# Two attentions worked by pairs of heads, four places for the weights of all: a one-core kernel of two transformer blocks

## The chip, the cores and the metric

One NeuronCore of a Trainium2 chip runs the whole program in one launch. Its engines run side by side and meet at semaphores: TensorE (PE, matmuls into PSUM), VectorE (DVE), ScalarE (ACT), GpSimd (POOL, hardly used here), and SyncE (SP), which issues the DMAs. The metric is the device time of one execution in microseconds, lower is better; the median of three runs stands for the kernel.

## The reference

Two blocks, each of two layers, on 256 tokens of width 1024, all in float32. A mixer is followed by a feed-forward part in each layer. The four mixers are these:

```
stick-breaking (16 heads of 64): z = q k^T / 8;  past = key < query
    log_fail = where(past, log_sigmoid(-z), 0);  later = reversed exclusive cumsum(log_fail)
    a = where(past, exp(log_sigmoid(z) + later), 0);  out = a v
dilated (8 heads of 64, three groups of dilation 1, 4, 16, 256 keys each): banded softmax,
    the groups joined by softmax of their log-sum-exp, which is one softmax over all their keys
latent (8 heads, q and k of width 96, v of 64): 256 context queries over 256 keys,
    and 256 main queries over 512 keys (context and main)
grouped-query (8 heads of 128, 2 key-value heads): 256 queries over 512 keys
```

## The kernel before

Activations are kept with the feature on the 128 partitions and the token along the free axis. Most of the time goes to projections ("linear" phases): a weight chunk comes by DMA into one of three places of `raw`, ScalarE copies it into `whi` (a rounded high part), VectorE subtracts it into `wlo` (the rest), and TensorE multiplies high and low parts. Phases follow one another in a list; every engine walks the same list in its own block of code (`@block.tensor`, `@block.scalar`, `@block.vector`), in an order written out by hand. `at(family, key)` names the semaphore and the value that tells of an event, `own()` the engine's own last event. A linear behind an attention waits until all three engines have ended that attention. During an attention no weight chunk is split, and hardly any DMA runs.

The attention phases are the kinds "stick" and "softmax". In both, PSUM's eight banks (`ps[:, b, :]`, 512 floats a partition) hold scores in the low banks and finished products in the high ones.

*stick* goes through 16 heads. TensorE: `z(hd)` computes the scores, keys on the partitions and queries along the free axis (256 + 128 columns, as later queries only see the second half of the keys), into bank hd % 4. ScalarE: `ex(hd)` takes Abs, Exp and Ln (L1369, L1371, L1375). VectorE: `fail(hd)` makes the fail terms in `sbf` (L1851, L1855). TensorE then adds the sums over later keys into the same bank, by three matmuls with constant triangles (tiles `sbf,squares` in the trace). ScalarE: Exp into `sba` (L1393). VectorE: `mask(hd)` (L1863). TensorE: `attend(hd)` multiplies with v into bank 4 or 5, the even head on partitions 0 to 63 and the odd head on 64 to 127. When a pair of heads is done, ScalarE's `high(pair)` (L1381) copies it into `uh` and VectorE's `low(pair)` (L1868) subtracts the rest into `ul`. `sbt`, `sbe`, `sbl`, `sbf` and `sba` have two places each. The scores and v matmuls read 64 rows or write 64 columns of the array.

*softmax* goes through units, each 128 queries of one head: 16 units in the dilated attention ("dil", 384 or 768 keys, masked), 32 in the latent one ("mla", 16 of 256 keys and then 16 of 512), 16 in the grouped-query one ("gqa", 512 keys). Queries stand on the partitions. For unit n: TensorE `scores` (two heads at a time but for gqa), VectorE `max_` (L1902 and L1904, or L1896 with mask), ScalarE `exp_` (L1413, with the row sum) into `pr`, VectorE `norm_` (L1911, L1913), TensorE `turn` (L984, transposes of 128 x 128), ScalarE `copy_` (L1425) into `pt`, TensorE `attend`, two heads at a time. After four units of mla, two heads are complete ("ends"): ScalarE `high_` (L1433), VectorE `low_` (L1920). `pr` has three places, `pt` four, `small` holds the maxima and sums in two sets. All fp32 matmuls go through `mm` (L686), which is why one line stands for them. ScalarE and VectorE work in this order:

```
ScalarE: exp_(0); for n: exp_(n+1), copy_(n), high_(n-3) where that unit ends a pair
VectorE: max_(0); for n: max_(n+1), norm_(n), low_(n-4) where that unit ends a pair
TensorE, mla: scores(0), scores(1); for pair m: turn x2, scores(m+2), attend(m-1)
```

## Time and profile before

| | us |
|---|---|
| median of 3 runs | 1884.77 (1883.54 to 1887.55) |
| the profiled execution | 1886.12 |
| its span, first to last instruction | 1884.3 |
| TensorE busy | 1747.8 (93%) |
| VectorE busy | 1245.6 (66%) |
| ScalarE busy | 878.5 (47%) |
| mean granted TensorE clock | 0.972 of full |

The profile is of one execution. Busy times count instructions that compute; a wait, or the issue of a DMA, is idle. PE's times are modelled from starts, so a busy PE isn't PE at its peak. In a window's row, the stretch and its length are followed by the busy us of PE, PEld (weight loads), DVE, ACT and POOL, each with its number of instructions, then PEclk, the DMA share and GB/s; PEclk is the share of the full TensorE clock of 2.4 GHz that was granted (0.50 is 1.2 GHz). In a timeline's row stand the start, the duration of the group that was merged into it, the engine, the line, and `out<-in` by tile name; the brackets give the idle time before it and who ended it. An fp32 matmul shows as two records.

### The profile page before, as it was taken

What the parts mean: (1) busy time and instruction counts of PE and PEld (TensorE: products, weight loads), DVE (VectorE), ACT (ScalarE), POOL (GpSimd) and SP (SyncE); (2) the same over time, 40 slices, a digit from 0 to 9 for tenths busy, and PEclk for the clock granted to TensorE, in tenths of its full rate; (3) what the DMA queues carried; (4) which work ended last, traced back from release to release, by engine and by line L of the source; (5) the groups of instructions that cost most, each with busy time, mean ns of one, the idle gap of its engine ahead of it and who ended that gap; (6) DMA issues with size and microseconds to landing.
All of it is one profiled execution on the core that took longest, in us unless ns stands there. A gap on an engine that the chain in (4) does not pass through costs nothing.

```text
span 1884.3 us, 25106 instructions
## 1 busy us (share of the span) xinstructions
PE 1747.8 (93%) x9870; PEld 1458.6 (77%) x9870; DVE 1245.6 (66%) x1539; ACT 878.5 (47%) x1113; POOL 0.2 (0%) x4
## 2 busy tenths in 40 slices
PE   6998999989997899988988799999999988999998
PEld 4876788978885688887656477887888876789997
DVE  4855778757885677855356646878566665577764
ACT  5464554454335455335535635333233354565552
POOL 0000000000000000000000000000000000000000
PEclk9999999989999899998998999999999989999999
DMA  5922367734650356743104022555644513035551
GB/s 178 309 80 90 121 193 240 245 111 160 220 183 1 117 181 203 230 135 104 36 17 129 1 95 85 170 164 175 229 157 145 190 60 125 1 117 194 183 184 63
DMA packets 240471, 264.75 MB, mean 141 GB/s; under 512 B 7007, under 2 KB 218978, under 8 KB 240354
## 3 DMA queue, kind: packets, MB, share of 16 engines
q1 hardware_dynamic: 238658, 258.90, 42.1%
q10 hardware_dynamic: 1696, 4.26, 0.7%
q8 instruction: 78, 1.28, 0.3%
q14 instruction: 39, 0.32, 0.1%
HBM read 262.08 MB, written 1.05 MB: 140 GB/s over the span
## 4 chain that ended last, share of the span: by engine, by line
PE 79%; DVE 10%; ACT 8%; issue 2%; DMA 1%; DVEq 0%; ACTq 0%
PE ps L686 77%; ACT y L1315 2%; DVE wlo L1492 1%; ACT u L1318 1%; PE ps L984 1%; ACT whi L1057 1%; DVE y L1779 1%; DVE u L1772 1%; DVE small L1902 1%; DMA xin<-in_ctx 1%; DVE y L1711 1%; DVE rstd L1675 1%; DVE rstd L1677 1%; DVE y L1796 1%; ACT pt L1425 1%
## 5 line engine op out<-in xcount | busy, mean ns | idle before, releaser
L686 PE MATMUL ps<-u,whi 128*128 128x512 f32 (+2 forms) x3408 | 899.3, 347 | 33.3 <-DVE u L1772 15.6
L686 PEld LDWEIGHTS ps<-u,whi 128*128 128x128 f32 (+1 forms) x3408 | 593.0, 192 | 135.6 <-issue 25.7
L686 PE MATMUL ps<-u,wlo 128*128 128x256 f32 (+1 forms) x2084 | 646.9, 310 | 0.0
L1492 DVE TENSOR_TENSOR wlo<-raw,whi 128x2048 fp32r<-128x2048 f32 (+6 forms) x212 | 454.1, 2142 | 227.4 <-ACT whi L1057 220.3
L1057 ACT ACTIVATE whi<-raw 128x2048 fp32r<-128x2048 f32 (+6 forms) x212 | 381.1, 1798 | 233.8 <-PE ps L686 214.9
L686 PEld LDWEIGHTS ps<-u,wlo 128*128 128x128 f32 x2084 | 399.2, 192 | 20.8
L686 PE MATMUL ps<-hid,whi 128*128 128x512 f32 (+1 forms) x1212 | 353.7, 364 | 0.0
L686 PE MATMUL ps<-hid,wlo 128*128 128x256 f32 (+1 forms) x864 | 261.9, 303 | 0.0
L686 PEld LDWEIGHTS ps<-hid,whi 128*128 128x128 f32 x1212 | 216.3, 189 | 40.6 <-issue 3.4
L686 PEld LDWEIGHTS ps<-hid,wlo 128*128 128x128 f32 x864 | 163.5, 189 | 7.0
L1711 DVE SCALAR_TENSOR_TENSOR y<-idle_half,cc,y 128x1024 f32<-128x1024 f32 x70 | 89.9, 1285 | 5.3 <-DVE wlo L1492 0.5
L1239 ACT ACTIVATE cacc<-ps,convv 128x512 f32<-128x512 f32 (+1 forms) x44 | 29.6, 674 | 107.2 <-PE ps L686 106.3
L686 PE MATMUL ps<-squares 128*128 128x256 f32 (+1 forms) x308 | 72.1, 388 | 0.0
L686 PE MATMUL ps<-sq,squares 128*128 128x256 f32 (+1 forms) x108 | 45.7, 577 | 26.5 <-ACT sq L1119 17.1
L686 PEld LDWEIGHTS ps<-squares 128*128 128x128 f32 x308 | 59.0, 194 | 9.8 <-issue 1.9
L686 PE MATMUL ps<-whi,u 128*128 128x512 f32 (+1 forms) x224 | 65.6, 374 | 0.0
L1156 ACT ACTIVATE work<-ps 128x512 f32<-128x512 f32 x38 | 22.7, 599 | 91.5 <-PE ps L686 91.4
L1249 ACT ACTIVATE csil<-cacc 128x512 f32<-128x512 f32 (+1 forms) x44 | 23.2, 528 | 87.6 <-PE ps L686 85.1
L984 PE MATMUL ps<-squares,pr 128*128 128x128 f32 x232 | 39.8, 296 | 23.5 <-DVE pr L1913 18.5
L1772 DVE TENSOR_TENSOR u<-y,u 128x256 fp32r<-128x256 f32 (+1 forms) x80 | 40.4, 505 | 26.7 <-ACT u L1318 21.7
L686 PEld LDWEIGHTS ps<-sq,squares 128*128 128x128 f32 x108 | 24.7, 251 | 42.8 <-issue 29.6
L1425 ACT ACTIVATE pt<-ps 128x512 f32<-128x512 f32 (+2 forms) x72 | 37.1, 515 | 42.9 <-PE ps L984 41.3
(228 smaller groups left out, 1617.0 us busy)
## 6 DMA issues: line engine op xcount, KB each, us to landing
raw<-in_ffn_w_up SPq DMA_DIRECT2D x44, 1024.0 KB, 5.1
raw<-in_w_ff_in SPq DMA_DIRECT2D x32, 1024.0 KB, 5.3
raw<-in_w_ff_out SPq DMA_DIRECT2D x32, 1024.0 KB, 5.2
modw<-in_w_mod SPq DMA_DIRECT2D x112, 256.0 KB, 3.8
idle_half<-in_w_mod SPq DMA_DIRECT2D x80, 256.0 KB, 3.4
raw<-in_w_in_dil SPq DMA_DIRECT2D x18, 1024.0 KB, 5.1
raw<-in_w_in_sb SPq DMA_DIRECT2D x12, 1024.0 KB, 7.4
raw<-in_w_ple_gate SPq DMA_DIRECT2D x8, 1024.0 KB, 5.2
```

The source lines that it names most:

```text
L686: return pe.matmul(out_, lhsT, rhs, start=start, stop=stop, skip_group_check=True)
L984: last = pe.transpose(ps[:, (4 + k // 4) if wide else 4 + n % 2, (k % 4) * P:(k % 4 + 1) * P], pr[:, n % 3, k * P:(k + 1) * P], ident)
L1057: nc.scalar.activation(whi[:, s % SPLIT, 0:n], raw[:, c["r"] % RAW, 0:n], ACT.Copy).then_inc(*up("weights_high", s))
L1156: nc.scalar.activation(half_sum(p, c), halves_of(c)[1], ACT.Copy, scale=HD ** -0.5 if kind == "qk1" and g < 4 else 1.0).then_inc(*up("half ...
L1239: nc.scalar.activation(cacc[:, j, 0:T], A_[:, j, :], ACT.Identity, bias=convv[:, l, 66 + f:67 + f], scale=convv[:, l, 22 + f:23 + f]).then ...
L1249: nc.scalar.activation(csil[:, j, 0:T], cacc[:, j, 0:T], ACT.Silu).then_inc(*up("gated_silu", (i, g - 1, j)))
L1315: nc.scalar.activation(y[:, k, sl], y[:, k, sl], ACT.Identity, bias=mod_at(l, which, k, s_), scale=mod_at(l, which + 1, k, s_)).then_inc(* ...
L1318: nc.scalar.activation(dst[:, k_, 0:p["T"]], y[:, p.get("s0", 0) + k, 0:p["T"]], ACT.Copy).then_inc(*up("operand_high", (i, k)))
L1425: nc.scalar.activation(pt[:, n % 4, c0:c0 + w], ps[:, (4 + c0 // 512) if u["mask"] is not None else 4 + n % 2, 0:w], ACT.Copy).then_inc(*u ...
L1492: nc.vector.tensor_tensor(wlo[:, s % SPLIT, 0:n], raw[:, c["r"] % RAW, 0:n], whi[:, s % SPLIT, 0:n].bitcast(F32), ALU.subtract).then_inc(* ...
L1711: nc.vector.scalar_tensor_tensor(total, mod_weights(m), cc[:, k, v:v + 1], total, ALU.mult, ALU.add).then_inc(*up("mod_taken", m["n"]))
L1772: nc.vector.tensor_tensor((cl if c else ul)[:, k_, 0:T], y[:, s0 + k, 0:T], (ch if c else uh)[:, k_, 0:T].bitcast(F32), ALU.subtract).then ...
```

## The change

In the stick-breaking attention TensorE's `z` and `attend` take a pair of heads j, the matmuls of the two heads alternating. Scores go through six banks and products into banks 6 and 7. `sbl` and `sbf` get three places, `sba` four. ScalarE runs `ex` two heads ahead of the weights' Exp where it ran one ahead, VectorE `fail` two ahead of `mask`. `high` and `low` of a pair come later: `high` after an even head, `low` after an odd one.

In the latent attention (`step = 2`) ScalarE does two `exp_`, then two `copy_`, then `high_` of the pair before; VectorE two `max_`, then `low_`, then two `norm_`; TensorE issues the scores of pair m + 2 ahead of the turns of pair m. The dilated and grouped-query attentions keep their order (`step = 1`). For all three `pr` gets a fourth place and `small` four sets, so `exp_` and `max_` wait for what lies four units back, not two or three. `pt` keeps four places, of which the fourth is now the tile `work`. No instruction is added or taken away.

```diff
-        sbl = arena("sbl", [P, 2, 384], 30 * K)
-        sbf = arena("sbf", [P, 2, 384], 33 * K)
-        sba = arena("sba", [P, 2, 384], 36 * K)
+        sbl = arena("sbl", [P, 3, 384], 30 * K)
+        sbf = arena("sbf", [P, 3, 384], 35 * K)
+        sba = arena("sba", [P, 4, 384], 40 * K)
...
-        pr = arena("pr", [P, 3, 768], 41 * K)
-        pt = arena("pt", [P, 4, 768], 50 * K)
+        pr = arena("pr", [P, 4, 768], 41 * K)
+        pt3 = arena("pt", [P, 3, 768], 53 * K)
...
+        pt = [pt3[:, n, :] for n in range(3)] + [work[:, :, :, :].rearrange("p a b c -> p (a b c)")]
+    def z(j):
+
+        for hd in (2 * j, 2 * j + 1):
+            if hd >= 6:
+                pe.wait_ge(*at("stick_weights", (i, hd - 6)))
+        for keys in range(2):
+            for hd in (2 * j, 2 * j + 1):
+                o, b = (hd % 2) * 64, hd % 6
+                qh = q1[o:o + 64, j, :]
+                if keys == 0:
+                    mm(ps[:, b, 0:256], k1[o:o + 64, j, 0:P], qh, True, False)
+                else:
+                    mm(ps[:, b, 256:384], k1[o:o + 64, j, P:S], qh[:, P:S], False, True).then_inc(*up("scores", (i, hd)))
+
+    def attend(j):
+
+        for hd in (2 * j, 2 * j + 1):
+            pe.wait_ge(*at("masked", (i, hd)))
+        if j >= 2:
+            pe.wait_ge(*at("operand_low", (i, j - 2)))
+        for keys in range(2):
+            for hd in (2 * j, 2 * j + 1):
+                o = (hd % 2) * 64
+                vv = v1[:, keys, hd * 64:(hd + 1) * 64]
+                if keys == 0:
+                    mm(ps[o:o + 64, 6 + j % 2, 0:256], vv, sba[:, hd % 4, 0:256], True, False)
+                else:
+                    mm(ps[o:o + 64, 6 + j % 2, 128:256], vv, sba[:, hd % 4, 256:384], False, True).then_inc(
+                        *up("attended", (i, hd)))
...
-    for hd in range(HEADS):
-        if hd + 2 < HEADS:
-            z(hd + 2)
...
-        if hd >= 1:
-            attend(hd - 1)
-    attend(HEADS - 1)
+    for j in range(HEADS // 2):
+        for hd in (2 * j, 2 * j + 1):
+            b, zb = hd % 3, hd % 6
+            pe.wait_ge(*at("fail_ready", (i, hd)))
+            mm(ps[:, zb, 0:256], negtri, sbf[:, b, 0:256], False, False)
+            mm(ps[:, zb, 128:256], negones, sbf[:, b, 256:384], False, False)
+            mm(ps[:, zb, 256:384], negtri, sbf[:, b, 256:384], False, True).then_inc(
+                *up("fail_summed", (i, hd)))
+        if j + 2 < HEADS // 2:
+            z(j + 2)
+        if j >= 1:
+            attend(j - 1)
+    attend(HEADS // 2 - 1)
...
-    ahead = 1 if wide else 4 // heads_of
+    ahead = dict(mla=2, dil=1, gqa=4)[p["what"]]
...
-        if wide and m + 1 < M:
-            scores(m + 1)
+        if p["what"] != "gqa" and m + ahead < M:
+            scores(m + ahead)
         for u in units[m * heads_of:(m + 1) * heads_of]:
             turn(u)
-        if not wide and m + ahead < M:
+        if p["what"] == "gqa" and m + ahead < M:
             scores(m + ahead)
...
-        if hd >= 2:
-            act.wait_ge(*at("fail_ready", (i, hd - 2)))
-        act.wait_ge(*own())
-        nc.scalar.activation(sbl[:, b, :], sbe[:, b, :], ACT.Ln, bias=1.0).then_inc(
+        if hd >= 3:
+            act.wait_ge(*at("fail_ready", (i, hd - 3)))
+        act.wait_ge(*own())
+        nc.scalar.activation(sbl[:, hd % 3, :], sbe[:, b, :], ACT.Ln, bias=1.0).then_inc(
             *up("weights_exp", (i, hd)))
...
     ex(0)
+    ex(1)
     for hd in range(HEADS):
-        if hd + 1 < HEADS:
-            ex(hd + 1)
-        b = hd % 2
+        if hd + 2 < HEADS:
+            ex(hd + 2)
         act.wait_ge(*at("fail_summed", (i, hd)))
-        if hd >= 2:
-            act.wait_ge(*at("attended", (i, hd - 2)))
-        act.wait_ge(*own())
-        nc.scalar.activation(sba[:, b, :], ps[:, hd % 4, 0:384], ACT.Exp).then_inc(*up("stick_weights", (i, hd)))
-        if hd % 2 == 1 and hd >= 3:
-            high(hd // 2 - 1)
+        if hd >= 4:
+            act.wait_ge(*at("attended", (i, hd - 4)))
+        act.wait_ge(*own())
+        nc.scalar.activation(sba[:, hd % 4, :], ps[:, hd % 6, 0:384], ACT.Exp).then_inc(*up("stick_weights", (i, hd)))
+        if hd % 2 == 0 and hd >= 4:
+            high(hd // 2 - 2)
+    high(HEADS // 2 - 2)
     high(HEADS // 2 - 1)
...
-        if n >= 3:
-            act.wait_ge(*at("turned", (i, n - 3)))
...
+        if n >= 4:
+            act.wait_ge(*at("turned", (i, n - 4)))
...
-    exp_(units[0])
-    for n in range(N):
-        if n + 1 < N:
-            exp_(units[n + 1])
-        copy_(units[n])
-        if n >= 3 and units[n - 3]["ends"]:
-            high_(units[n - 3])
-    for n in (N - 3, N - 2, N - 1):
-        if units[n]["ends"]:
-            high_(units[n])
+    step, lag = (2, 1) if p["what"] == "mla" else (1, 3)
+    for u in units[0:step]:
+        exp_(u)
+    for n in range(0, N, step):
+        for u in units[n + step:n + 2 * step]:
+            exp_(u)
+        for u in units[n:n + step]:
+            copy_(u)
+        if n >= lag and units[n - lag]["ends"]:
+            high_(units[n - lag])
+    for u in units[N - lag:]:
+        if u["ends"]:
+            high_(u)
...
-        if hd >= 2:
-            dve.wait_ge(*at("fail_summed", (i, hd - 2)))
...
+        if hd >= 3:
+            dve.wait_ge(*at("fail_summed", (i, hd - 3)))
...
     past2 = squares[:, 7:8, :].to_broadcast([P, 2, P])
     fail(0)
+    fail(1)
     for hd in range(HEADS):
-        if hd + 1 < HEADS:
-            fail(hd + 1)
+        if hd + 2 < HEADS:
+            fail(hd + 2)
         mask(hd)
-        if hd % 2 == 0 and hd >= 4:
+        if hd % 2 == 1 and hd >= 5:
             low(hd // 2 - 2)
     low(HEADS // 2 - 2)
     low(HEADS // 2 - 1)
...
-        if n >= 2:
-            dve.wait_ge(*at("weights_exp", (i, n - 2)))
+        if n >= 4:
+            dve.wait_ge(*at("weights_exp", (i, n - 4)))
         if u["mask"] is not None:
-            if n >= 3:
-                dve.wait_ge(*at("turned", (i, n - 3)))
+            if n >= 4:
+                dve.wait_ge(*at("turned", (i, n - 4)))
...
-    max_(units[0])
-    for n in range(N):
-        if n + 1 < N:
-            max_(units[n + 1])
-        norm_(units[n])
-        if n >= 4 and units[n - 4]["ends"]:
-            low_(units[n - 4])
-    for n in (N - 4, N - 3, N - 2, N - 1):
-        if units[n]["ends"]:
-            low_(units[n])
+    step, lag = (2, 3) if p["what"] == "mla" else (1, 4)
+    for u in units[0:step]:
+        max_(u)
+    for n in range(0, N, step):
+        for u in units[n + step:n + 2 * step]:
+            max_(u)
+        if step == 2 and n >= lag and units[n - lag]["ends"]:
+            low_(units[n - lag])
+        for u in units[n:n + step]:
+            norm_(u)
+        if step == 1 and n >= lag and units[n - lag]["ends"]:
+            low_(units[n - lag])
+    for u in units[N - lag:]:
+        if u["ends"]:
+            low_(u)
```

Old `z` and `attend` stand above. The rest renames places in the same way (`n % 3` to `n % 4`, `hd % 4` to `hd % 6`, `pt[:, n % 4, ...]` to `pt[n % 4][...]`, the columns of `small`, banks 4 and 5 to 6 and 7).

## Rows read from the trace of the kernel before

**Rows 1.** The page's chain that ended last: share of the span by engine.

```profile
PE 79%; DVE 10%; ACT 8%; issue 2%; DMA 1%; DVEq 0%; ACTq 0%
```

**Rows 2.** Busy us per engine in three attention stages: stick-breaking, latent, grouped-query.

```profile
105.20:155.70 50.50, 45.91 (x224) 33.97 (x225) 25.93 (x56) 36.16 (x73) 0.00 (x0) 0.93 0.05 18
...
1019.70:1089.40 69.70, 56.78 (x352) 34.69 (x352) 46.35 (x138) 40.88 (x105) 0.00 (x0) 0.88 0.04 15
1608.30:1648.00 39.70, 36.92 (x226) 27.65 (x227) 27.34 (x72) 26.03 (x57) 0.00 (x0) 1.00 0.00 1
```

**Rows 3.** Timeline, stick-breaking: ScalarE's first instruction, then one head (start, us, what).

```profile
106.19 0.49 ACT L1369 ACTIVATE sbt<-ps 128x384 f32<-128x384 f32 x1 [1.07 <-PE ps L686]
...
126.59 0.38 ACT L1381 ACTIVATE u<-ps 128x256 fp32r<-128x256 f32 x1
126.69 0.92 PE L686 MATMUL ps<-q,k 64*128 64x256 f32 x4
127.07 0.49 ACT L1369 ACTIVATE sbt<-ps 128x384 f32<-128x384 f32 x1
127.54 1.14 PE L686 MATMUL ps<-sbf,squares 128*128 128x256 f32 x6
...
128.61 0.86 PE L686 MATMUL ps<-sba,v 128*64 128x256 f32 x4
...
128.84 0.49 ACT L1393 ACTIVATE sba<-ps 128x384 f32<-128x384 f32 x1
...
129.41 0.92 PE L686 MATMUL ps<-q,k 64*128 64x256 f32 x4
129.43 0.49 ACT L1369 ACTIVATE sbt<-ps 128x384 f32<-128x384 f32 x1
```

**Rows 4.** Windows with the granted clock (PEclk): stick-breaking, dilated, latent.

```profile
109.50:116.00 6.50, 6.50 (x20) 4.74 (x19) 2.81 (x6) 3.67 (x8) 0.00 (x0) 0.50 0.00 0
...
575.00:600.00 25.00, 18.02 (x188) 13.79 (x186) 15.34 (x50) 16.81 (x38) 0.00 (x0) 1.00 0.00 1
1022.00:1033.80 11.80, 11.01 (x36) 7.03 (x34) 7.86 (x30) 6.55 (x21) 0.00 (x0) 0.50 0.03 9
```

**Rows 5.** Timeline of VectorE, latent stage, one 512-wide unit.

```profile
1064.43 0.69 DVE L1902 TENSOR_REDUCE small<-ps 128x1 f32<-128x512 f32 x1
...
1065.41 0.16 DVE L1911 RECIPROCAL small<-small 128x1 f32<-128x1 f32 x1
...
1066.23 0.69 DVE L1902 TENSOR_REDUCE small<-ps 128x1 f32<-128x512 f32 x1
```

**Rows 6.** The maxima's line between 1047 and 1084: duration ns min/median/max, first and last start.

```profile
L1902 DVE TENSOR_REDUCE small<-ps x16: 691/692/693, 1047.3 to 1082.9; 128x1 f32<-128x512 f32 x16
```

**Rows 7.** Who waited for whom between 1047 and 1084: us, times, longest.

```profile
DVE u L1920 <- ACT u L1433: 6.9, 4, 2.7
```

**Rows 8.** Timeline of TensorE, latent stage, one pair of 512-wide units.

```profile
1064.84 1.88 PE L686 MATMUL ps<-km,qm 96*128 96x512 f32 x4
1066.65 1.09 PE L686 MATMUL ps<-pt,vm 128*64 128x128 f32 x16
1067.68 1.09 PE L984 MATMUL ps<-squares,pr 128*128 128x128 f32 x8
1068.61 1.88 PE L686 MATMUL ps<-km,qm 96*128 96x512 f32 x4
```

**Rows 9.** Timeline of TensorE, stick-breaking: first scores, then the slow start.

```profile
105.26 1.54 PE L686 MATMUL ps<-q,k 64*128 64x256 f32 x12 [1.21 <-ACT v L1182]
108.90 1.64 PE L686 MATMUL ps<-sbf,squares 128*128 128x256 f32 x6 [2.09 <-DVE sbf L1855]
...
112.04 2.07 PE L686 MATMUL ps<-sbf,squares 128*128 128x256 f32 x6
114.04 1.54 PE L686 MATMUL ps<-sba,v 128*64 128x256 f32 x4
```

**Rows 10.** The chain in order of time: the last Ln of stick-breaking.

```profile
149.92 0.53 ACT sbl L1375
```

More of the change, by code:

```diff
@@ L918, in attend @@
-                    def attend(hd):
-                        b = hd % 2
-                        pe.wait_ge(*at("masked", (i, hd)))
-                        pair, o = hd // 2, (hd % 2) * 64
-                        if pair >= 2 and hd % 2 == 0:
-                            pe.wait_ge(*at("operand_low", (i, pair - 2)))
-                        dst = ps[o:o + 64, 4 + pair % 2, 0:S]
-                        vv = [v1[:, t, hd * 64:(hd + 1) * 64] for t in range(2)]
-                        mm(dst[:, 0:256], vv[0], sba[:, b, 0:256], True, False)
-                        mm(dst[:, 128:256], vv[1], sba[:, b, 256:384], False, True).then_inc(
-                            *up("attended", (i, hd)))
@@ L983, in turn @@
                         for k in range(kt):
-                            last = pe.transpose(ps[:, (4 + k // 4) if wide else 4 + n % 2, (k % 4) * P:(k % 4 + 1) * P], pr[:, n % 3, k * P:(k + 1) * P], ident)
+                            last = pe.transpose(ps[:, (4 + k // 4) if wide else 4 + n % 2, (k % 4) * P:(k % 4 + 1) * P], pr[:, n % 4, k * P:(k + 1) * P], ident)
                         last.then_inc(*up("turned", (i, n)))
@@ L1424, in copy_ @@
                             act.wait_ge(*own())
-                            nc.scalar.activation(pt[:, n % 4, c0:c0 + w], ps[:, (4 + c0 // 512) if u["mask"] is not None else 4 + n % 2, 0:w], ACT.Copy).then_inc(
+                            nc.scalar.activation(pt[n % 4][:, c0:c0 + w], ps[:, (4 + c0 // 512) if u["mask"] is not None else 4 + n % 2, 0:w], ACT.Copy).then_inc(
                                 *up("turned_copied", (i, n)))
@@ L1900, in max_ @@
+                                    -u["scale"], small[:, 8 + b:9 + b] if c0 else -NEG, ALU.add, ALU.min,
+                                    accum_out=small[:, b:b + 1] if c0 + w == W else small[:, 8 + b:9 + b]).then_inc(*up("max_ready", (i, n)))
                         else:
                             dve.wait_ge(*own())
-                            nc.vector.tensor_reduce(small[:, 4 + b:5 + b], ps[:, n % 4, 0:W], AX.X, ALU.max).then_inc(*up("vector_step"))
+                            nc.vector.tensor_reduce(small[:, 8 + b:9 + b], ps[:, n % 4, 0:W], AX.X, ALU.max).then_inc(*up("vector_step"))
```

51 lines of the change are left out of this document (16 added, 35 removed).

## The prediction

> **What bounds the kernel now.** I read the page's chain first: TensorE holds 79% of it [rows 1], so time is won only where TensorE waits, or where it is shortened itself. Then the busy time of the attention stages [rows 2], which are all that the change touches. Outside them nothing is edited; inside them the DMA share is 0 to 5%, so no transfer can be late. The grouped-query stage has TensorE busy 36.9 of 39.7 us: it is bound there. The others have it idle or at the lower clock for part of the time: stick-breaking 45.9 of 50.5 at a mean clock of 0.93, latent 56.8 of 69.7 at 0.88, and the dilated one 18.0 of the 25 in its middle [rows 4].
>
> In the stick-breaking stage the timelines [rows 3] give the steady state. TensorE runs scores (126.69), tail sums (127.54), products with v (128.61) and the next scores (129.41) without a break: 2.72 us a head, 5.43 a pair. ScalarE's own work is a little less: Abs, Exp and Ln take 1.77 (127.07 to 128.84), the weights' Exp 0.59 (to 129.43), and the copy of a finished pair 0.48 (126.59 to 127.07). That is 2 x 2.36 + 0.48 = 5.20 a pair. So TensorE bounds, with ScalarE 4% behind. At the start it is slower: the clock stands at 1.2 GHz from 109.5 to 116 [rows 4], after TensorE had stood from the end of the first scores (106.8) to 108.9 for head 0's Ln and fail terms [rows 9].
>
> In the latent stage VectorE sets the pace of the 512-wide units: max and its scaling 0.98 (1064.43 to 1065.41), reciprocal and scaling 0.82 (to 1066.23), so 1.80 a unit [rows 5]. But the sixteen maxima from 1047.3 to 1082.9 [rows 6] lie 2.37 apart. The waits say where the rest is: 6.9 us in four waits for ScalarE's copy of a finished pair [rows 7]. That copy waits for the products with v, and these stand on TensorE behind the scores: scores 1.81, products 1.03, two turns 0.93 [rows 8], 3.77 a pair.
>
> **The change part by part.** *Stick-breaking, TensorE.* The matmuls of two heads now alternate and use different halves of the array (64 rows for the scores, 64 columns for v). The trace shows the effect already: the scores of heads 0, 1 and 2, issued one after the other, took 1.54 us for three [rows 9], not 3 x 0.85. Two overlapped and one alone give about 0.7 + 0.85. I take 0.85 for a pair of scores (a wait included) and 0.85 for a pair's products, and 1.07 for each tail sum: 3.84 a pair. Bounds: no overlap at all, 2 x (0.85 + 1.07 + 0.80) = 5.43 less two waits saved; full overlap, 3.8. Below 5.20 ScalarE is the bound, so even poor overlap leaves most of the gain.
>
> *Stick-breaking, ScalarE.* Six score banks, three places for Ln and for the fail terms and four for the weights let ScalarE run two heads ahead. Between the end of a head's Ln and its weights' Exp now lie about 4.7 us of other ScalarE work; the path through VectorE (1.0) and TensorE (1.1, or 2.0 at the lower clock) is shorter, so ScalarE should not wait. It starts at 106.19 [rows 3]. Up to the end of the last Ln it has 16 x 1.77 + 13 x 0.59 + 5 x 0.48 = 38.4 us, so 144.6. Walking the first heads with the matmuls at 1.2 GHz (tail sums 2.0, 112.04 to 114.04; scores about as the products of one head, 1.5; [rows 9]) adds 0.3: 144.9. Now it is 149.92 + 0.53 = 150.45 [rows 10]: 5.5 us gained. From there to the next linear at 155.7 the chain is the same (fail terms, sums, Exp, mask, products, copy, subtraction), plus one thing: the subtraction of pair 5 now stands behind the mask of head 15 on VectorE, and the last products wait for it, +0.5. **Stick-breaking: -5.0.** Of it 1.3 to 1.9 is the steady state (0.12 a head), the rest the idle of ScalarE at the start. Bounds: -1 (waits eat the lead) and -6.
>
> *Stick-breaking, the clock.* TensorE will be busy 3.84 of 5.20 us, 74%, in pieces with waits of up to about a microsecond. The nearest rows are the dilated stage: busy 18.0 of 25 us (72%) from 575 to 600, with the granted clock at 1.00 [rows 4], that is 2.4 GHz. I take it to hold. The Trainium skill, "TensorE: Matmul & The Clock Gate", section "A second HAM failure mode: psum-queue depth-cycling", speaks against this: small idles between groups that cycle through PSUM banks can make the clock swing between its levels. The dilated row does not show it there, but such a drop comes in the rows of other stages; what it would cost is the last rival.
>
> *Latent.* Two maxima, then the subtraction, then two norms; two exponentials, then two copies; scores ahead of the turns. The work is the same, instruction for instruction. The copy of a finished pair now comes while VectorE does the next two maxima (2 x 0.98), which covers turn, copy and products after the norms (0.5 + 0.6 + 1.0). So four 512-wide units cost 4 x 1.80 + 0.56 (subtraction with its gaps) + 0.1 left of the wait = 7.9, or 1.97 a unit; TensorE's 3.77 a pair stays just under 3.94. From unit 16's maximum to unit 30's: 14 x 1.97 = 27.6, and to unit 31's 28.6, where now it is 35.6. The end gets longer: after the last maxima come two norms of the pair before (1.6), then the subtraction waits for turn, copy, products and copy (2.5) with no maxima to cover it, then the last two norms (1.6), turn, copy, products, copy, subtraction (3.5). From unit 31's maximum to the next linear that is 10.3; now 1089.4 - 1082.8 = 6.6. So -7.0 + 3.7 = -3.3. In the 256-wide half TensorE runs at 1.2 GHz until 1033.8, busy 11.0 of 11.8 us [rows 4]: the order can change nothing much. After it about two waits for the pair's copy go, at half of the 1.7 us (6.9 / 4) that they cost above: -1.7 at most, 0 at least; I take -1.2 for both and the order at the start. **Latent: -4.5**, between 0 (the lengthened end and new waits eat it) and -7.
>
> *Dilated and grouped-query.* Order and work stay. Four places for the weights let a maximum start before the turn of three units back. By VectorE's order that turn has nearly always ended by then, so I allow **-0.2**, between 0 and -1: the maxima of the stage are few (16), and each could come earlier only until it waits for its scores. Grouped-query is bound by TensorE, whose work is untouched: 0. What hides the moved fourth place of the turned weights is nothing: it is an address. If a linear's use of that tile met the attention, it would wait; the stages are apart.
>
> Sum: 5.0 + 3.3 + 1.2 + 0.2 = 9.7. The profiled execution took 1886.12 (span 1884.3, 1.8 around it), so 1876.4; it lies 1.35 above the median 1884.77, so **1875** for the median. Behind each stage comes a linear that waits for it, with TensorE as its bound, so the gain should pass through whole.
>
> **Rivals.** *The latent stage gives nothing.* The subtraction stands before the norms and waits for a copy that waits for products; if that wait (2.5 us without cover, at the end) shows between the pairs too, 0.6 us a pair over the eight wide pairs eats the 4.5. For: TensorE and VectorE are within 4% of each other, so there is no slack to catch up. Against: the maxima cover 2.0 of it. Time: 1884.8 - 5.2 = 1879.6.
> *The stick-breaking stage gives little.* VectorE takes fail (hd+2) before mask (hd), so a late Ln holds the mask, the products and the bank. Against: VectorE has 25.9 of 50.5 us to do. With -1 there: 1879.1; with the latent stage at nothing as well, 1883.6, which is no change.
> *Slower: the clock.* If with more idle TensorE stays at 1.2 GHz in the stick-breaking stage, a pair costs 2 x 2.0 for the tail sums and 2 x 1.5 for scores and products (a head's took 1.54 at that clock, and an overlapped pair takes about as long as one head) [rows 9]: 7.0 instead of 5.20. Eight pairs from 108.9, where the first tail sums start, end at 164.9, and the next linear comes at 166.1 instead of 155.7, +10.4; with -4.7 elsewhere 1890.5. For: it fell there before. Against: it came back at 116 with the same instructions running back to back, as they will again. Each pair at the lower clock costs 1.8; with six the whole gain is gone, with eight the kernel is slower by over 0.2%.
>
> **How the numbers follow.** Both stages gain as above: 0.64, times 1871 to 1879. Latent at nothing 0.16 (1879.6), stick-breaking at little 0.08 (1879 to 1881), both at nothing 0.06 (about 1884), the clock 0.06 (1890.5). Beyond the likeliest the range takes the two one-sided cases, up to 1881; its lower end is both stages at their better bounds, -6 and -7 with some gain in the clock, near 1870. 0.2% (3.8 us) is about what a measurement of this kernel can tell from no change; 1881.0 is that border. Faster: 0.64 + 0.16 + about half of the third case = 0.84; same 0.10; slower 0.06.
>
> **What would show it.** Stick-breaking: next linear near 150.6, ScalarE without idle before its Exp (L1393's line) from 107 on, TensorE with 0.5 to 1 us of idle a pair; two score matmuls starting within 0.05 us. Latent: wide maxima in twos, 3.9 us from pair to pair, VectorE's waits for the pair's copy under 2 us in all but for one at the end; stage 65 instead of 69.7 long. Grouped-query unchanged to 0.2. Wrong if: pairs over 5.3 us in the first, a granted clock of 0.5 there after 117, or a wait of over 0.6 us for the copy at each second pair.

## The result, and the profile after

The changed kernel takes 1873.68 us, the median of six runs (1872.44 to 1875.26); the kernel before took 1884.15 beside it (1882.09 to 1887.55). The ratio is 0.9943, with a 95% interval from 0.993 to 0.9956: faster by 10.5 us. The prediction was 1875, in a range from 1870 to 1881.

The profiled execution took 1872.93 us, with a span of 1871.1: 13.2 less than the profiled span before. That pair overstates the gain, as the profiled execution of before lay 2.0 above its median and that of after 0.75 below its own: 13.2 - 2.75 = 10.5. Since durations come from the profiles, the terms below are compared there.

Windows of the stick-breaking and the latent stage, to be read beside [rows 2]:

```profile
105.00:149.70 44.70, 32.51 (x224) 25.15 (x225) 25.91 (x56) 36.02 (x73) 0.00 (x0) 0.96 0.06 20
...
1010.30:1073.50 63.20, 54.91 (x352) 33.24 (x352) 46.33 (x138) 40.74 (x105) 0.00 (x0) 0.95 0.05 16
```

In the stick-breaking stage TensorE's busy time fell from 45.9 to 32.5 us with the same instructions, VectorE's and ScalarE's did not move, and the stage is 5.8 shorter. In the latent stage all busy times stay about as they were (56.8 to 54.9 for TensorE, at a higher clock): what went is idle time.

A stage is measured in the traces from TensorE's first instruction in it to the first one of the next linear:

| us | before | after | difference | predicted |
|---|---|---|---|---|
| stick-breaking | 50.46 | 44.69 | -5.77 | -5.0 |
| latent: first maximum to the 17th | 25.90 | 22.42 | -3.48 | -1.2 |
| latent: 17th maximum to the 32nd | 35.56 | 28.73 | -6.83 | -7.0 |
| latent: 32nd maximum to the next linear | 6.60 | 10.41 | +3.81 | +3.7 |
| latent, whole | 69.72 | 63.23 | -6.49 | -4.5 |
| dilated | 49.21 | 49.03 | -0.18 | -0.2 |
| grouped-query | 39.27 | 39.23 | -0.04 | 0 |

That is 12.5 of the 13.2. The other 0.7 is what is left of larger differences in stretches that were not edited: the linears between the dilated and the latent stage took 405.4 us where they had taken 409.1, those between the latent and the grouped-query one 521.4 against 518.9. The same 409.1 came down to 405.5 in a kernel below with the old latent attention (`stick_only`), so this is scatter. The dilated stage scatters too: with the new places and one and the same list it took from 46.0 to 51.3 us in the kernels below, its mean granted clock being 0.96 and 0.80 there. Its -0.18 says nothing.

**Stick-breaking.** Timeline after, one pair of heads and ScalarE's first instruction, to be read beside [rows 3]:

```profile
105.96 0.49 ACT L1378 ACTIVATE sbt<-ps 128x384 f32<-128x384 f32 x1 [1.07 <-PE ps L687]
...
123.23 0.49 ACT L1402 ACTIVATE sba<-ps 128x384 f32<-128x384 f32 x1
...
124.22 1.14 PE L687 MATMUL ps<-sbf,squares 128*128 128x256 f32 x6 [1.29 <-DVE sbf L1868]
...
125.29 0.92 PE L687 MATMUL ps<-q,k 64*128 64x256 f32 x8
...
126.15 0.87 PE L687 MATMUL ps<-sba,v 128*64 128x256 f32 x8
...
128.41 0.49 ACT L1402 ACTIVATE sba<-ps 128x384 f32<-128x384 f32 x1
```

The scores of two heads now take 0.92 us, as those of one did before (x8 against x4 records for the same duration); their products take 0.87. From 123.23 to 128.41 is the period of a pair: 5.18, where TensorE's loop gave 5.43. TensorE now waits (1.29 before the sums at 124.22), and ScalarE does not. The bound has passed from TensorE to ScalarE.

The chain at the end of the same stage (start, us, engine, tile and line):

```profile
143.33 0.53 ACT sbl L1384
...
146.66 0.43 DVE sba L1876
...
147.19 0.44 DVE u L1881
...
147.76 0.89 PE ps L687 x8
...
149.73 0.47 PE ps L687
```

The last Ln ends at 143.86, against 150.45 before [rows 10]. Behind it the mask (146.66) is followed by the subtraction of an earlier pair (147.19), and only then come the last products.

**Latent.** Timeline of VectorE, one pair of 512-wide units: two maxima, the first of two norms, and the next pair's maximum:

```profile
1046.01 0.69 DVE L1916 TENSOR_REDUCE small<-ps 128x1 f32<-128x512 f32 x1
...
1047.02 0.69 DVE L1916 TENSOR_REDUCE small<-ps 128x1 f32<-128x512 f32 x1
...
1048.00 0.16 DVE L1925 RECIPROCAL small<-small 128x1 f32<-128x1 f32 x1
...
1049.60 0.69 DVE L1916 TENSOR_REDUCE small<-ps 128x1 f32<-128x512 f32 x1
```

In such a step nothing but the instructions' own gaps is left: 3.59 a pair. Every other step has the subtraction too, and takes 4.13 to 4.48 from 1041.9 on: 0.56 for the subtraction, up to 0.46 for a wait for ScalarE's copy. The maxima's line in two stretches (number, ns min/median/max, first and last start), and the wait for the pair's copy from 1034 to 1072, which answers to [rows 7]:

```profile
L1916 DVE TENSOR_REDUCE small<-ps x17: 423/425/692, 1012.0 to 1034.4; 128x1 f32<-128x256 f32 x16, 128x1 f32<-128x512 f32 x1
...
L1916 DVE TENSOR_REDUCE small<-ps x15: 691/692/692, 1035.4 to 1063.1; 128x1 f32<-128x512 f32 x15
...
DVE u L1934 <- ACT u L1443: 3.1, 3, 2.2
```

The 512-wide maxima lie (1063.1 - 1034.4) / 15 = 1.91 apart, 2.37 before [rows 6]. Of the waits for the copy one long one is left, 2.2 us. It stands in the lengthened end, which the chain shows in order of time:

```profile
1063.13 0.70 DVE small L1916
...
1065.10 0.50 DVE pr L1927
...
1067.40 0.39 ACT u L1443
...
1067.82 0.43 DVE u L1934
...
1069.33 0.50 DVE pr L1927
...
1073.55 0.47 PE ps L687
```

From the norm's end at 1065.60 the chain leaves VectorE for turns, products and copy and comes back at 1067.82 for the subtraction. The last two norms start only behind it. That they could have started earlier is shown below, by the kernel that does them first.

**The clock.** Windows of after (the slow stretch of stick-breaking, its middle, the slow stretch of the latent stage), then the slow stretch of the latent stage before, beside [rows 4]:

```profile
110.50:113.90 3.40, 3.40 (x15) 2.60 (x15) 1.96 (x4) 2.96 (x6) 0.00 (x0) 0.50 0.00 0
...
116.00:142.00 26.00, 20.11 (x148) 15.26 (x147) 16.33 (x36) 22.27 (x46) 0.00 (x0) 1.00 0.01 1
...
1011.70:1018.40 6.70, 6.37 (x16) 4.45 (x16) 5.05 (x19) 3.77 (x13) 0.00 (x0) 0.50 0.19 64
```

```profile
1020.80:1034.40 13.60, 12.20 (x43) 8.06 (x44) 9.38 (x34) 6.83 (x22) 0.00 (x0) 0.50 0.12 42
```

From 116 to 142 the stick-breaking stage keeps 2.4 GHz with TensorE busy 20.1 of 26 us. In the latent stage the clock is back after 6.8 us (at 1018.4), where it took 13.7 before.

### The profile page after: what moved, and what is told of

It is laid out like the page before. It is cut to its first block, busy times and chain, and to the rows that moved or that the text cites. A ratio compares the mean times of both kernels' runs of the same rounds, so it can differ in the third digit from the quotient of the medians.

```text
span 1871.1 us, 25111 instructions
## 1 busy us (share of the span) xinstructions
PE 1732.7 (93%) x9870; PEld 1449.5 (77%) x9870; DVE 1245.3 (67%) x1539; ACT 876.8 (47%) x1113; POOL 0.2 (0%) x4
## 4 chain that ended last, share of the span: by engine, by line
PE 77%; DVE 10%; ACT 9%; issue 2%; DMA 1%; DVEq 0%; ACTq 0%
PE ps L687 75%; ACT y L1324 2%; DVE wlo L1505 1%; ACT u L1327 1%; PE ps L993 1%; ACT whi L1066 1%; DVE y L1792 1%; DVE u L1785 1%; DVE pr L1927 1%; DVE small L1916 1%; DVE y L1724 1%; DMA xin<-in_ctx 1%; DVE rstd L1688 1%; DVE rstd L1690 1%; DVE y L1809 1%
## 5 line engine op out<-in xcount | busy, mean ns | idle before, releaser
L993 PE MATMUL ps<-squares,pr 128*128 128x128 f32 x232 | 39.7, 295 | 18.3 <-DVE pr L1927 12.5
L1595 DVE SCALAR_TENSOR_TENSOR cacc<-ps,convv,cacc 128x510 f32<-128x510 f32 (+1 forms) x44 | 27.1, 615 | 43.8 <-ACT cacc L1248 40.8
```

The source lines that it names most:

```text
L993: last = pe.transpose(ps[:, (4 + k // 4) if wide else 4 + n % 2, (k % 4) * P:(k % 4 + 1) * P], pr[:, n % 4, k * P:(k + 1) * P], ident)
L1595: nc.vector.scalar_tensor_tensor(a[:, :, 1:S], x[:, :, 0:S - 1], convv[:, l, f:f + 1], a[:, :, 1:S], ALU.mult, ALU.add).then_inc(*up("vect ...
```

## The experiments

Twelve kernels were run, each timed against the kernel before on the same chip. "Stage" is the length as in the table above.

**Each half alone.** The first kernel has the new stick-breaking attention and the old softmax attentions, the second the reverse.

> The change in the stick-breaking attention alone; the softmax attentions as before. If the stages gain apart from each other, the stick-breaking stage is 44.7 us long as after (50.5 before), the latent stage stays at 69 to 70, and the time is 5.8 us under before. If the earlier return of the clock or the earlier end in one stage helps the other, the latent stage shortens here too, by 1 us or more.

> The change in the softmax attentions alone; stick-breaking as before. If the stages gain apart, stick-breaking stays at 50.5 us, the latent stage is 63.2 as after (69.7 before), and the time is 6.5 us under before. The rival, that half of the latent gain is the clock's phase and not the order, gives 65 to 68 for the latent stage here, since the stage starts 5.8 us later.

```diff
# stick_only: the softmax attentions' lists as before
+                    max_(units[0])
+                    for n in range(N):
...
# latent_only: stick's lists, places and banks as before
-                        if hd + 2 < HEADS:
-                            ex(hd + 2)
+                        if hd + 1 < HEADS:
+                            ex(hd + 1)
```

Stick-breaking alone: 1878.89, ratio 0.9968 (0.9952 to 0.9984), its stage 45.50, the latent one 69.67. Latent alone: 1881.79, 0.9982 (0.9967 to 0.9996), its stage 63.23 to the hundredth as in the full change, stick-breaking 50.48. In the profiles the halves don't touch each other, and the ratios multiply to 0.995, within the interval of the full change. The times are less clear than the stages: the first half gives 6.2 us against the 1885.04 beside it, as expected (5.8), the second 3.3 where its stage gives 6.5 and 6.5 was expected; even the end of its interval, 0.9967, is only 6.2. Single times of that kernel run from 1871.3 to 1884.6, and no run tells where the rest went.

The first kernel's stick-breaking stage is 0.8 longer than the full change's (45.50 against 44.69), though the same lists run there. The last Ln ends as long after ScalarE's first instruction in both (37.9); the difference lies behind it, where in this run the clock fell, and not at the start:

```profile
109.90:145.40 35.50, 25.91 (x182) 20.02 (x182) 21.72 (x48) 30.48 (x63) 0.00 (x0) 1.00 0.01 1
145.40:148.80 3.40, 3.22 (x16) 2.11 (x17) 1.90 (x5) 1.09 (x3) 0.00 (x0) 0.50 0.00 0
```

There everything waits for TensorE's last sums and products, which no other work covers.

**A lead of one head, not two.** Banks, places and pairs stay; only ScalarE and VectorE run one head ahead as before.

```diff
-                    ex(1)
...
-                        if hd + 2 < HEADS:
-                            ex(hd + 2)
+                        if hd + 1 < HEADS:
+                            ex(hd + 1)
...
-                    fail(1)
...
-                        if hd + 2 < HEADS:
-                            fail(hd + 2)
+                        if hd + 1 < HEADS:
+                            fail(hd + 1)
```

> After, with ScalarE and VectorE one head ahead in stick-breaking as they were before; TensorE's pairs, banks and places stay. If the gain is ScalarE's lead of two heads, ScalarE waits again for the tail sums (VectorE 1.0 and TensorE 1.1 to 2.8 against 2.4 to 2.8 of its own work): a pair costs 5.4 to 6.2 us instead of 5.2 and the stage 47 to 53. If the gain is TensorE's shorter work by pairs, the lead doesn't matter and the stage stays under 46.

1875.9, ratio 0.9955 (0.9936 to 0.9975), stage 48.34. Timeline of ScalarE's weights' Exp in the slow start, in the middle and for the last head, and windows of the two stretches at the lower clock:

```profile
115.34 0.49 ACT L1401 ACTIVATE sba<-ps 128x384 f32<-128x384 f32 x1 [1.34 <-PE ps L687]
...
122.86 0.49 ACT L1401 ACTIVATE sba<-ps 128x384 f32<-128x384 f32 x1
...
128.05 0.49 ACT L1401 ACTIVATE sba<-ps 128x384 f32<-128x384 f32 x1
...
149.07 0.49 ACT L1401 ACTIVATE sba<-ps 128x384 f32<-128x384 f32 x1 [2.13 <-PE ps L687]
```

```profile
109.20:116.00 6.80, 6.36 (x22) 5.20 (x23) 3.34 (x8) 4.55 (x10) 0.00 (x0) 0.50 0.00 0
...
146.70:150.10 3.40, 3.14 (x14) 2.35 (x14) 1.06 (x3) 0.73 (x2) 0.00 (x0) 0.50 0.00 0
```

The stage came out as expected, the pair did not: the steady pair takes 5.19 with either lead, so one head is enough at 2.4 GHz. Of the 3.65 us by which the stage is longer than after's, part is the clock of this run. It was down for 6.8 us at the start, where after had 3.4; the kernel `low_after`, further down, has the lead of two and the same 6.8, and takes 45.03. And it fell again from 146.7 on, which by the end of the stage (6.80 from the last Ln to the next linear, 5.88 in after) costs some 0.9. That leaves about 2.4 for the second head of lead, an estimate. ScalarE's waits tell where: with one head of lead it waits 2.4 us before the first three weights' Exp (0.59, 0.44 and 1.34), with two heads and the same 6.8 us at the lower clock 0.5 (`low_after`); the other 0.6 lies at the end, where the last head's work starts later.

**Pairs without alternation.** The new loops, but each head's two matmuls issued together.

```diff
-                        for keys in range(2):
-                            for hd in (2 * j, 2 * j + 1):
+                        for hd in (2 * j, 2 * j + 1):
+                            for keys in range(2):
```

> After, with the scores and the products with v of a pair issued head by head, not alternating. If the two halves of the array overlap without alternation, as the first three scores of before seem to show (1.54 us for three), nothing changes: stage 44.7. If overlap needs the alternation, a pair of scores takes 1.3 to 1.6 us instead of 0.85; ScalarE then still bounds (TensorE about 5.0 of 5.2 us a pair), and the stage grows by under 2 us.

1873.48, ratio 0.994 (0.9924 to 0.9956), stage 44.73. Timeline, one pair:

```profile
125.31 0.93 PE L687 MATMUL ps<-q,k 64*128 64x256 f32 x8
...
126.17 0.88 PE L687 MATMUL ps<-sba,v 128*64 128x256 f32 x8
```

0.93 and 0.88 where alternation gives 0.92 and 0.87. The two halves of the array overlap in either order; what counts is that nothing stands between the two heads.

**Is it order or clock?** Matmuls with unused results were put ahead of the first tail sums and of the latent scores, in the kernels after and before.

```diff
+            def idle(n):
+                for _ in range(n):
+                    mm(ps[:, 5, 0:S], ones, squares[:, 0:2, :].rearrange("p j c -> p (j c)"), True, True)
...
                     z(1)
+                    idle(4)
...
+                    if p["what"] == "mla":
+                        idle(6)
```

> After, with idle matmuls (results unused) in the two places where TensorE stands ahead of the stages: 4 after the first scores of stick-breaking, 6 ahead of the first scores of the latent stage; they are there to keep the clock at 2.4 GHz. If stick-breaking is bound by ScalarE even while the clock is down, its stage stays at 44.7 (within 0.4) although the clock stays up. In the latent stage TensorE bounds while the clock is down (1012 to 1018), so it is 1 to 3 us shorter. If the matmuls don't hold the clock, nothing changes.

> The same idle matmuls in the kernel before. There TensorE bounds stick-breaking, so a clock that stays up gives 3 to 4 us in that stage (50.5 to about 47) and 2 to 5 in the latent one (69.7). If stick-breaking before was held by something else at its start, it gains under 1 us. It also tells how much of the change's gain was the time at the lower clock: the change should be worth only about 2 us in stick-breaking against this kernel.

Windows of the stick-breaking stage, after with idle matmuls, then before with them:

```profile
104.90:149.60 44.70, 33.12 (x232) 25.56 (x233) 25.93 (x56) 36.04 (x73) 0.00 (x0) 1.00 0.06 21
```

```profile
104.30:151.60 47.30, 44.68 (x233) 33.34 (x233) 25.93 (x56) 36.11 (x73) 0.00 (x0) 1.00 0.05 19
```

Both hold the full clock throughout. After stays at 44.69: the 3.4 us at the lower clock in its own run had cost nothing, as ScalarE bounds there too. Before falls from 50.46 to 47.29. So 2.6 of the gain of 5.8 is order at the full clock, and 3.2 is what the lower clock at the start had cost the old order. The new order is nearly, but not wholly, proof against it: in `low_after` and `turns_first`, below, the same stick-breaking lists ran with 6.8 us at the lower clock, as in before, and took 45.03 and 45.04. The window of the former:

```profile
110.10:116.90 6.80, 6.38 (x25) 5.02 (x24) 4.12 (x10) 5.68 (x12) 0.00 (x0) 0.50 0.01 2
```

In the latent stage the idle matmuls did harm, against both expectations: 65.06 and 71.09. The clock fell later instead of earlier, and in after with idle matmuls for longer:

```profile
1016.90:1027.10 10.20, 9.94 (x39) 6.12 (x38) 6.54 (x24) 5.12 (x17) 0.00 (x0) 0.50 0.01 2
```

Whole kernels: 1875.85, ratio 0.9935 (0.9919 to 0.9952), and 1880.38, 0.996 (0.9944 to 0.9976).

A second try spread idle matmuls over the first pairs of the latent stage, so as to keep its clock up in both kernels.

```diff
                     for m in range(ahead):
+                        if p["what"] == "mla":
+                            idle((6, 1)[m])
                         scores(m)
+                    if p["what"] == "mla":
+                        idle(3)
...
                             attend(m - 1)
+                        if p["what"] == "mla" and m < 3:
+                            mm(ps[:, 7, 0:S], ones, squares[:, 0:2, :].rearrange("p j c -> p (j c)"), True, True)
```

> After, with idle matmuls in TensorE's gaps of the first narrow units of the latent stage (6 ahead of the first scores, 1 between, 3 behind, 1 in each of the first three steps), to keep the clock at 2.4 GHz there. If the clock stays up, the narrow part (first to seventeenth maximum) is 21.5 to 22.4 us (22.4 after): VectorE bounds it. The idle matmuls themselves may cost up to 1 us.

> The same idle matmuls in the kernel before. If half of what the change gained in the narrow part (25.9 to 22.4) is the clock, which came back after 6 instead of 13 us, the narrow part is 23.5 to 24.5 here. If all of it is the order, it stays near 25.9 with the clock up; if all is the clock, it is 22.4.

After: 1875.91, 0.9948 (0.993 to 0.9967), stage 64.64; its first half is 22.43, at the full clock, where after has 22.42 with the low one for 6.8 us near its start. So that half is bound by VectorE, and that fall costs it nothing. (The later and longer fall of the first try did cost: 24.22.) The stage is still 1.4 longer than after's, all of it in the end (11.80 against 10.41), where the clock now fell for 3.4 us from 1068.7. Before: 1886.72, 1.0012 (0.9997 to 1.0028), stage 67.52, first half 25.37. Windows of the latter:

```profile
1019.70:1035.00 15.30, 13.10 (x76) 9.45 (x78) 11.59 (x38) 8.34 (x27) 0.00 (x0) 1.00 0.18 62
1035.00:1040.00 5.00, 3.46 (x24) 2.18 (x20) 3.91 (x16) 2.68 (x9) 0.00 (x0) 0.78 0.00 0
```

The attempt was only partly clean: the clock fell at 1037.8 for 3.4 us, and the pair behind it took 5.10 us, where the same pair of the kernel before takes 3.67 at full clock. Without the 1.4, the old order at full clock takes 23.9, an estimate. Of the 3.5 that the first half gained, then, 25.9 - 23.9 = 2.0 had been the clock's and 23.9 - 22.4 = 1.5 the order's.

**One engine's order alone.** In the latent stage first TensorE's old order (turns ahead of scores) under the new lists of the others, then the reverse.

```diff
# turns_first
-                        if p["what"] != "gqa" and m + ahead < M:
+                        if wide and m + ahead < M:
                             scores(m + ahead)
...
-                        if p["what"] == "gqa" and m + ahead < M:
+                        if not wide and m + ahead < M:
                             scores(m + ahead)
# scores_first
-                    step, lag = (2, 1) if p["what"] == "mla" else (1, 3)
+                    step, lag = 1, 3
...
-                    step, lag = (2, 3) if p["what"] == "mla" else (1, 4)
+                    step, lag = 1, 4
```

> After, with TensorE's order in the latent stage as before: turns, scores two pairs ahead, products; ScalarE and VectorE stay at pairs. If TensorE's order is a needed part of the gain, the scores now come behind the turns of norms that VectorE does after two maxima, VectorE waits about 1.4 us a pair for scores, and the stage is 66 to 72 us long. If only the order on ScalarE and VectorE matters, it stays at 63 to 64.

> After, with ScalarE's and VectorE's order in the latent stage as before (one unit at a time) and TensorE's scores ahead of the turns: the other half of the latent edit alone. If the two orders only work together, each copy waits behind scores and holds the next exponential, the scores wait for that one, and a wide pair takes about 5.1 us instead of 4.6 before and 3.9 after: stage 72 to 76. If TensorE's order alone brings the products forward and with them the pair's copy, a pair takes 3.9 and the stage 60 to 63.

Turns first: 1899.37, ratio 1.0063 (1.0047 to 1.0079), slower than before, stage 91.61. Scores first: 1906.75, 1.0117 (1.0099 to 1.0136), stage 95.17. The latent window of the first, and its timeline of both engines around one pair:

```profile
1008.70:1100.30 91.60, 69.18 (x353) 39.98 (x353) 46.32 (x138) 40.80 (x105) 0.00 (x0) 0.74 0.03 11
```

```profile
1064.08 0.69 DVE L1916 TENSOR_REDUCE small<-ps 128x1 f32<-128x512 f32 x1 [1.61 <-PE ps L687]
...
1066.82 1.45 PE L993 MATMUL ps<-squares,pr 128*128 128x128 f32 x8 [0.89 <-DVE pr L1927]
1068.10 1.88 PE L687 MATMUL ps<-km,qm 96*128 96x512 f32 x4
...
1069.16 0.69 DVE L1916 TENSOR_REDUCE small<-ps 128x1 f32<-128x512 f32 x1 [1.61 <-PE ps L687]
```

A closed ring: the turns wait for the norms (0.89), the scores stand behind the turns, and the next two maxima wait for these scores (1.61). This pair takes 5.08. Every second pair has the subtraction too; two of these that ran at full clock take 5.61 and 5.95. The other kernel has a ring of its own, in which the scores wait for an exponential that ScalarE runs too late; its latent window and a start of scores:

```profile
1014.40:1109.60 95.20, 68.73 (x352) 43.58 (x353) 46.34 (x138) 40.78 (x105) 0.00 (x0) 0.73 0.03 11
```

```profile
1074.51 1.95 PE L687 MATMUL ps<-km,qm 96*128 96x512 f32 x4 [2.29 <-ACT pr L1423]
```

There a pair takes 5.02 at full clock, and one in which a copy and a subtraction fall due 6.79 (from the maximum at 1067.48 to the one at 1074.27). So in the mean a pair takes longer than the 5.0 and 5.1 on which the expectations went, and the stages are longer than their upper ends, 72 and 76. Two things had been left out: these pairs, and the clock, at 0.74 and 0.73 in the mean. The clock's part can't be told apart exactly. TensorE is busy 14.3 and 13.8 us longer than in after for the same instructions (54.91 there); if that is what the lower clock adds, an estimate, then no more than half of the 28.4 and 31.9 us by which the stages are longer than after's is the clock, and the rest is waits. VectorE's and ScalarE's orders and TensorE's gain only together.

**The subtraction and its wait.** First the subtraction is put behind the norms throughout, then only in the last step of the latent stage, with stick-breaking's last-but-two subtraction ahead of the last mask.

```diff
# low_after
-                        if step == 2 and n >= lag and units[n - lag]["ends"]:
-                            low_(units[n - lag])
                         for u in units[n:n + step]:
                             norm_(u)
-                        if step == 1 and n >= lag and units[n - lag]["ends"]:
+                        if n >= lag and units[n - lag]["ends"]:
                             low_(units[n - lag])
# tails
+                        if hd == HEADS - 1:
+                            low(hd // 2 - 2)
                         mask(hd)
-                        if hd % 2 == 1 and hd >= 5:
+                        if hd % 2 == 1 and 5 <= hd < HEADS - 1:
                             low(hd // 2 - 2)
...
-                        if step == 2 and n >= lag and units[n - lag]["ends"]:
+                        ahead_of_norm = step == 2 and n + step < N
+                        if ahead_of_norm and n >= lag and units[n - lag]["ends"]:
                             low_(units[n - lag])
...
-                        if step == 1 and n >= lag and units[n - lag]["ends"]:
+                        if not ahead_of_norm and n >= lag and units[n - lag]["ends"]:
                             low_(units[n - lag])
```

> After, with VectorE's subtraction of a finished pair behind the two norms in every step of the latent stage, not ahead of them. The steps with a subtraction take 4.46 us after (3.6 without); 0.56 of it is the subtraction, 0.3 the rest of the wait for ScalarE's copy. If the wait is real, it goes: 4.16, the wide part 1 us shorter (28.7 to 27.7) and the end 8.4 instead of 10.4, stage about 60.2. If TensorE is by then the bound of these steps, they stay at 4.4 and only the end gains (61.2).

> After, with the last pair's subtraction moved in both stages: in the latent one behind the last two norms, in stick-breaking the subtraction of pair 5 ahead of the mask of head 15. By the prediction's steps this takes the uncovered wait (about 2.2 us) out of the latent end and 0.5 us out of the stick-breaking end: stages 61.0 and 44.2 instead of 63.2 and 44.7. If the ends are bound elsewhere (ScalarE's copies, TensorE), neither moves by over 0.3.

Behind throughout: 1870.99, ratio 0.9927 (0.9912 to 0.9943), latent stage 62.31, of which 28.41 in the 512-wide part (28.73 after) and 9.81 at the end (10.41). Of the 1.0 expected in the wide part only 0.3 came, in one step. There had been waits to remove, 0.46 and 0.41 us for the copy in two steps of after. The second is gone; in place of the first a wait of 0.46 stands ahead of a norm (1054.89), and the profile names no other engine that ended it. The end got 0.6 shorter and not the 2.0 of the kernel below. The clock fell in it (a fall there cost 1.4 in two other kernels, 11.8 against 10.41); a window of this kernel's last units:

```profile
1070.00:1075.60 5.60, 4.47 (x47) 3.60 (x43) 0.85 (x2) 2.53 (x5) 0.00 (x0) 0.76 0.00 0
```

Only in the last step: **1870.65, ratio 0.9899 (0.9882 to 0.9917)**, latent stage 61.23, its end 8.40, stick-breaking 44.57. The chain at the end of both stages:

```profile
145.95 0.43 DVE sba L1876
...
146.48 0.43 DVE u L1881
...
147.01 0.44 DVE sba L1876
...
1069.34 0.16 DVE small L1920
...
1070.59 0.50 DVE pr L1929
```

In the latent stage the last norms now follow the last maxima at once (1069.34, then 1070.59), and 2.0 us are gone. In stick-breaking the move gave 0.12: mask, subtraction and mask stand back to back from 145.95 on, so the subtraction has only changed its place in a full queue. This version is faster than the kernel before, and its ratio's interval lies below that of the change, though the two were not run side by side. The medians differ by 3.0 us (1873.68 and 1870.65), of which the stages explain 2.1; the kernel before stood at 1886.72 beside it, 2.6 higher than beside the change, so the ratio flatters it a little.

## Why the prediction was right, point by point

**What bounds.** Right for both stages, in their steady state. Stick-breaking passed from TensorE at 5.43 a pair to ScalarE at 5.18 (predicted 5.20); the latent wide part to VectorE, whose maxima take 27.7 us from the 17th to the 31st (predicted 27.6).

**Stick-breaking, -5.0: measured -5.77.** From ScalarE's first instruction to the end of the last Ln were predicted 144.9 - 106.19 = 38.7 and came 143.86 - 105.96 = 37.9. The instructions add up to 0.5 less. The 0.3 of waits from the walk did not come either, but only because the clock of this run was down for 3.4 us. The walk had the first heads' matmuls at the lower clock as in before, where it was down for 6.8, and the two kernels with 6.8 have these waits: 0.35 longer to the last Ln, stage 45.03 and 45.04. The end was put at +0.5: it is (149.73 - 143.86) - (155.7 - 150.45) = +0.6. That two heads overlap without alternation was the reading of [rows 9], and the run without it bears that out. The prediction gave 1.3 to 1.9 of the gain to the steady state and the rest to the start; with the full clock throughout, the kernels differ by 2.6, so the rest, 3.2, was the price of the lower clock at the start.

**The clock there.** Held where the prediction looked, as taken from the dilated row: 20.1 busy of 26 at 1.00. The Trainium skill ("TensorE: Matmul & The Clock Gate", section "A second HAM failure mode: psum-queue depth-cycling"), which was weighed against it, tells of a bf16 kernel whose clock swings between its levels as TensorE idles shortly between groups that cycle through PSUM banks. No swing shows from 116 to 142 here. But the forecast held with some luck: in two kernels with the same stick-breaking lists, `stick_only` and `scores_first`, the clock fell for 3.4 us from 145.4 and 145.2, which the prediction had named as a sign of being wrong (0.5 after 117). It cost 0.8 and 0.9 us of stage, not the 1.8 a pair of the rival. In the two kernels with one engine's order alone the clock did swing: TensorE busy 69.2 of 91.6 and 68.7 of 95.2, and a mean of 0.74 and 0.73.

**Latent, wide part -7.0 and end +3.7.** Measured -6.83 and +3.81. The first is right partly by luck: before's 35.56 holds a fall of the clock for 3.4 us from 1054.9, and with idle matmuls in the stage's first pairs, where that fall is absent, it is 33.92; the order is then worth 5.2, and some 1.6 is the clock. The prediction put the whole 7.0 down to the order. The end is right in size and in cause: moving the subtraction there gave 2.0 back.

**Latent, first half -1.2: measured -3.5.** This is the term that was mis-sized most. The step read "the order can change nothing much" while TensorE is at 1.2 GHz. It took the length of that stretch as given. With the new order the clock is back after 6.8 us instead of 13.7, and that is no chance of one run: it is 6.8 in all six profiled kernels that have both halves of the new latent order and no idle matmuls, 13.7 in both with the old one. About 2.0 of the 3.5 is that clock; the remaining 1.5 is order, near the 1.7 that was the upper bound set for it. Taken together, order alone is worth 5.2 + 1.5 - 3.8 = 2.9 us of the latent stage's 6.5, less than the 4.5 predicted for it; the other 3.6 is time at the lower clock, which the prediction put at nothing.

**Rivals.** That the latent stage gives nothing is refuted by the run of its half alone (6.5 us of stage; of the time only 3.3, 0.9982). That stick-breaking gives little, likewise (0.9968). A stick-breaking stage that stays at the slower clock did not occur.

**The sum.** 9.7 predicted, 12.5 in the stages of the profiled pair and 10.5 by the medians, with an interval from 8.3 to 13.2. The closeness of 9.7 and 10.5 is in part luck: two shares of the clock, 2.0 and 1.6, were left out, and the latent order was put 1.6 too high. What stays open is what brings the clock back so much earlier in the latent stage, as idle matmuls moved its falls but gave no rule, and why the latent half alone gave so little of the time.

## What to carry to other kernels

When two engines walk hand-written lists, change both sides in one step: here either half of the latent change, by itself, closed a ring of waits and made the kernel slower, and the two together made it faster. Look at the last step of a software pipeline by itself: a wait that later work covers in the loop has no cover there, and moving one instruction in the last step gave 2 us. A lead that the steady state doesn't need may still pay where a stage starts at the lower clock: here 1.8 us of wait at the start. Before a stage's gain is put down to an order, look at the granted clock of both kernels in that stage.

## What the hardware showed that was not expected

- Matmuls that read 64 rows, or write 64 columns, overlap with their neighbours on the other half in plain issue order: 0.93 us for two heads' scores one after the other, 0.92 alternating.
- The granted clock does not follow TensorE's busy share alone. At 77% (20.1 of 26 us, with waits of 0.5 to 1.3 us) it stayed at 1.00; at 76% (69.2 of 91.6, with waits that repeat in every pair) it was 0.74 in the mean. Part of those 69.2 is the slower clock itself, so the share at equal clock is lower.
- The same instructions meet different falls from kernel to kernel. With one and the same stick-breaking lists the clock was down for 3.4 us at the start (after), for 6.8 (`low_after`), or not there but for 3.4 at the end (`stick_only`). The stage took 44.69, 45.03 and 45.50: a fall costs where no other work covers TensorE.
- Idle matmuls ahead of a stage moved the fall rather than preventing it in the latent stage (0.50 from 1016.9 to 1027.1, where after had it from 1011.6 to 1018.4), while four of them held the stick-breaking stage at 1.00 from end to end.
